# Second block of a two-block transformer kernel: the differential attention between the products that make its queries and values

## The reference

```python
def hybrid_attention_mixer(x, w_in, w_out, ...):
    proj = x @ w_in                                   # 1024 x 3072
    qa, ka, va, qb, kb, vb = split(proj)
    qa, ka, qb, kb = rms_norm of each, head by head (64 columns), times a gain
    oa = dilated_mixture_attention(qa, ka, va, slopes[:8])      # 8 heads of 64
    ob = differential_attention(qb, kb, vb, slopes[8:], lam)    # 4 heads: softmax(first) - lam * softmax(second), values 128 wide
    ob = rms_norm_2(ob, b_sub_norm) * (1.0 - lam_init)
    return concatenate([oa, ob]) @ w_out
```

## Time and profile before

| | |
|---|---|
| median of 3 runs | 2969.36 us (2969.0 to 2969.45) |
| span of the profiled execution | 2970.8 us |
| the profiled execution's own time beside it | 2970.8 us is all that is shown of it |
| TensorE busy | 2918.5 us, 98% |
| VectorE, ScalarE, GpSimd busy | 41%, 44%, 49% |
| mean granted TensorE clock | 0.995 of full |
| QKV products begin, product with w_out begins (profile) | 1759.89 us, 1979.10 us |

### The profile page before, as it was taken

The page is one execution under the profiler, slowest core; times in us unless marked ns, Lnnn a source line. Parts: engine busy times, 40 slices in busy tenths (PEclk is TensorE's granted clock), DMA queues, the critical chain, the costliest instruction groups (busy, mean ns, idle before and its releaser), DMA issues.

```text
span 2970.8 us, 39991 instructions
## 1 busy us (share of the span) xinstructions
PE 2918.5 (98%) x14264; PEld 2390.9 (80%) x14264; DVE 1232.9 (41%) x2085; ACT 1294.6 (44%) x2013; POOL 1449.4 (49%) x822
## 2 busy tenths in 40 slices
PE   8999999999989999999999999999999999999999
PEld 7878887888878778888888878668888887888887
DVE  5546434221063556433222160664555128455510
ACT  4556544222253556444223353654444237444421
POOL 4665555444444755555444454534444442444443
PEclk9999999999999999999999999999999999999999
DMA  4222232333322222333333323103333333233333
GB/s 143 73 86 78 86 121 85 99 98 100 106 78 86 75 96 65 100 114 100 96 99 99 107 78 92 58 8 101 97 99 93 99 94 92 92 98 99 93 108 89
DMA packets 77271, 273.32 MB, mean 92 GB/s; under 512 B 8776, under 2 KB 9416, under 8 KB 77152
## 3 DMA queue, kind: packets, MB, share of 16 engines
q1 hardware_dynamic: 74112, 266.05, 28.7%
q10 hardware_dynamic: 3040, 5.64, 0.5%
HBM read 269.55 MB, written 2.10 MB: 91 GB/s over the span
## 4 chain that ended last, share of the span: by engine, by line
PE 91%; DVE 4%; ACT 2%; issue 1%; POOL 1%; DMA 1%; SPq 0%; DVEq 0%; ACTq 0%; POOLq 0%
PE ps L737 25%; PE ps L739 25%; PE ps L738 25%; PE ps L1013 2%; PE ps L1038 2%; PE ps L1230 1%; PE ps L1231 1%; PE ps L1236 1%; PE ps L995 1%; DMA WRAW<-wall 1%; PE ps L1127 1%; POOL WLO L2689 1%; PE ps L1121 1%; PE ps L1122 1%; PE ps L990 0%
## 5 line engine op out<-in xcount | busy, mean ns | idle before, releaser
L2689 POOL TENSOR_TENSOR WLO<-WRAW,WHI 128x1024 fp32r<-128x1024 f32 x463 | 1116.3, 2414 | 1243.9 <-ACT WHI L1398 1243.9
L737 PE MATMUL ps<-HH,WHI 128*128 128x512 f32 x2184 | 857.2, 392 | 1.4 <-POOL WLO L2689 1.2
L739 PE MATMUL ps<-HH,WLO 128*128 128x512 f32 x2184 | 850.3, 389 | 0.0
L738 PE MATMUL ps<-HL,WHI 128*128 128x512 f32 x2184 | 850.0, 389 | 0.0
L1398 ACT ACTIVATE WHI<-WRAW 128x1024 fp32r<-128x1024 f32 x467 | 491.7, 1054 | 324.9 <-DMA WRAW<-wall 324.2
L737 PEld LDWEIGHTS ps<-HH,WHI 128*128 128x128 f32 x2184 | 410.0, 188 | 90.0 <-issue 4.8
L739 PEld LDWEIGHTS ps<-HH,WLO 128*128 128x128 f32 x2184 | 409.9, 188 | 86.3
L738 PEld LDWEIGHTS ps<-HL,WHI 128*128 128x128 f32 x2184 | 410.2, 188 | 82.7
L2535 DVE SCALAR_TENSOR_TENSOR ps<-U,COLS,ps 128x512 f32<-128x512 f32 x192 | 145.1, 756 | 121.2 <-ACT ps L1852 107.1
L2071 DVE TENSOR_TENSOR ACC<-ACC,SQ 128x512 f32<-128x512 f32 x80 | 70.5, 881 | 286.4 <-ACT SQ L1688 271.1
L737 PE MATMUL ps<-F2H,WHI 128*128 128x512 f32 x384 | 149.4, 389 | 0.0
(11 more groups left out here) (398 smaller groups left out, 4678.7 us busy)
## 6 DMA issues: line engine op xcount, KB each, us to landing
WRAW<-wall SPq DMA_DIRECT2D x502, 512.0 KB, 3.5
y<-X ACTq DMA_DIRECT2D x8, 256.0 KB, 3.9
X<-xin SPq DMA_DIRECT2D x3, 512.0 KB, 7.8
DFT<-dft ACTq DMA_DIRECT2D x4, 258.0 KB, 4.3
PT_IN<-pin ACTq DMA_DIRECT2D x2, 512.0 KB, 3.7
DIL<-dil ACTq DMA_DIRECT2D x1, 768.0 KB, 4.2
X<-xin SPq DMA_DIRECT2D x2, 256.0 KB, 4.8
COLS<-cols ACTq DMA_DIRECT2D x1, 290.5 KB, 5.5
```

The costliest lines, as they stand in the source:

```text
L737: pe.matmul(out_, WHI[w_at], x_hi, start=first, stop=False)
L738: pe.matmul(out_, WHI[w_at], x_lo, start=False, stop=False)
L739: return pe.matmul(out_, WLO[w_at], x_hi, start=False, stop=last)
L2689: pool.tensor_tensor(WLO[:, s, :], whole, WHI[:, s, :].bitcast(F32), ALU.subtract).then_inc(wt_lo, 1)
```

## The change

What it does, by engine:

- The columns of w_in are regrouped. The chunks are now: queries and keys of differential heads 0 and 1, then of heads 2 and 3, the differential values, queries and keys of dilated heads 0 to 3, then 4 to 7, and the dilated values (`QK_TILES`, "attn_w_in_2 by heads").
- `qkv` is one stage of 24 units without a loop. Its 96 steps (unit by token tile, six products each) are numbered, and tables of step numbers say between which products a piece of other work stands. All 16 differential pairs are scored, transposed and multiplied there, their norm is done head by head, and the scores of 8 of the 16 dilated pairs too. `alone` holds the last 8 dilated pairs, with the first half of four w_out tiles, now the differential half, between them.
- The order of pairs is turned round: differential first.
- The head norms are taken chunk by chunk: GpSimd's power (128 x 16, eight times) replaces square root and reciprocal, and the factors lie in SBUF (FQ) instead of PSUM.
- Within the products, all transposes (tiles, maps, spread factors) and the sums of squares use the one bank ps6, each waiting until the one before it was read (`turn_free`); from pair 20 on, second maps use ps3. All output goes to bank ps7 instead of two banks. Scores have two banks up to pair 24, four after it (before: four).
- The maps' buffers: 16 turned maps instead of 8, half of them in the parts of QKV that are no longer needed.

The core of the diff (`qkv` and `alone` as TensorE has them; `head_factors` is GpSimd's, `normed` VectorE's):

```diff
-TURNED = 8
+TURNED = 16
+QK_TILES = [f for a, h in ((8, 0), (8, 2), (0, 0), (0, 2)) for f in (a + h, a + h + 4, a + h + 1, a + h + 5)]
+QK_TURNED = by_step(24, 25, 26, 27, 40, 41, 42, 43, 73, 74, 75, 76, 89, 90, 91, 92)
+SCORED = by_step(27, 29, 32, 34, 37, 39, 42, 44, 47, 49, 52, 54, 57, 59, 62, 64, 77, 78, 80, 82, 85, 87, 89, 95)
+DIFF_TURNED = by_step(33, 35, 38, 39, 44, 45, 48, 50, 53, 55, 58, 60, 63, 65, 68, 70)
+SUMMED, SPREAD = by_step(57, 62, 69, 79), by_step(61, 67, 72, 82)
...
             def qkv(st):
+                att = st.att
+                opening_rows(st)
+                for m in range(CHUNK_STEPS, STEPS_QKV):
+                    j, s = divmod(m, ST)
+                    if m in QK_TURNED:
+                        turn_qk(att, QK_TURNED[m])
+                    if m in MAP_TURNED:
+                        turn_free(att, ("map", MAP_TURNED[m]))
+                        turn_map(att, *MAP_TURNED[m])
+                    if m in SUMMED:
+                        out_sums(att, SUMMED[m])
+                    if m in SPREAD:
+                        out_spread(att, SPREAD[m])
+                    if m in SCORED:
...
+                        scores(att, SCORED[m])
+                    for q in MULTIPLIED.get(m, ()):
...
+                        value_products(att, q)
...
+                    rows_done(st, j, s, rows_of(st, j, s, (j % 4 * 2, j % 4 * 2 + 1)))
+                alone(st, att, st.res)
...
+            def alone(st, att, res):
+                scores(att, ALONE)
+                rows_copied(st, CHUNK_VA)
+                turn_map(att, ALONE - 4, 1)
+                for k in range(ALONE, 32 + 4):
+                    if ALONE < k < 32:
+                        scores(att, k)
+                    if k < 32 + 3:
+                        turn_free(att, ("map", (k - 3, 0)))
+                        turn_map(att, k - 3, 0)
...
+                    if k == 26:
+                        half_tile(res, 0, 0, 2)
...
+            def head_factors(st, c, half_):
...
+                pool.tensor_tensor(FQ[:, at], VQ[:, at], NEGH[:, :], ALU.pow).then_inc(S["qk_factors_ready"], 1)
...
+            def normed(st, c, s):
...
+                f = FQ[:, head_sums(4 * c, s)].rearrange("p (a o) -> p a o", o=1).to_broadcast([P, 8, HD])
+                dve.tensor_tensor(v, v, f, ALU.mult).then_inc(S["qk_normed"], 1)
```

More of the change, by code:

```diff
@@ L289, in attention @@
     def attention(mode, groups, out, **opt):
-        pairs, host = groups * ST, opt.get("made")
+        pairs, host = groups * ST, opt["made"]
         n = 2 * pairs
[L292 to L296, removed]
+        per = {k: n for k in ("scores_ready", "exp_ready", "probs_turned", "turned_copied", "probs_ready")}
@@ L362, in plan @@
     n = norm("X", DM, "columns")
[L363 to L371, removed]
+    v = add("qkv", 1, 24, 24, {"rows_multiplied": 6 * (ST - 1)}, op=op, norm=n)
+    v.op_hi = op_hi
+    v.att = banded()
+    v.res = residual("O2", DT, "ffn_norm_20")
+    v.res.halves = True
     def conv_ffn(l, gain):
@@ L606, in turned_at, with turn_bank, out_tile, previous_turn @@
                 return {"gqa": PTG, "mla": PT}[st.mode][:, n % 4, :]
[L607 removed]
+            i = n % TURNED
+            return PT2[:, i, :] if i < 8 else QKV[:, i % 4, (i - 8) // 4 * SEQ:((i - 8) // 4 + 1) * SEQ]
+        def turn_bank(st, n):
+            if carried(st):
+                return turn_ps[n % 2]
+            return ps[3] if n % 2 and pair_of_map(st, n) >= ALONE - 4 else ps[6]
         def score_bank(st, q, c):
[L610 removed]
+            return ps[4 + c] if carried(st) or q <= ALONE or q % 2 == 0 else ps[1 + c]
         def out_bank(st, g):
[L613 removed]
+            return ps[st.made.heads_bank()] if carried(st) else ps[7]
+        def out_tile(g):
+            return DIL_H // 2 + g if g < DIFF_H else g - DIFF_H
+        def previous_turn():
+            order, before = [], {}
+            for m in range(CHUNK_STEPS, STEPS_QKV):
+                for kind, table in (("tile", QK_TURNED), ("map", MAP_TURNED), ("sum", SUMMED), ("spread", SPREAD)):
+                    if m in table:
+                        order.append((kind, table[m]))
+            order += [("map", (q, 0)) for q in range(ALONE - 3, 32)]
+            for a, b in zip(order, order[1:]):
+                before[b] = a
+            return before
+        BEFORE = previous_turn()
+        def turn_read(st, use):
+            kind, n = use
+            if kind == "map":
+                return copied(st, map_at(st, *n))
+            return {"tile": "qk_placed", "sum": "out_mean_ready", "spread": "out_scaled"}[kind], n + 1
         def query_hi(h):
@@ L979, in scores @@
                 a, b = spans(st.mode, t)
-                if not carried(st) and q == 1:
-                    for c in range(2):
-                        pe.wait_ge(bank_free[st.bank(2 + c)], st.use(2 + c))
-                if q >= (1 if carried(st) else 2):
+                if st.mode == "banded" and t == 0:
+                    i = 2 * g + 1
+                    pe.wait_ge(S["qk_placed"], st.at("qk_placed", i + 1))
+                if q:
                     pe.wait_ge(*scores_free(st, q))
```

621 lines of the change are left out of this document (317 added, 304 removed).

## The result

The changed kernel takes 2974.56 us (median of 20 runs, 2972.69 to 2977.26), the kernel before 2970.61 (20 runs on the same chip, 2968.47 to 2972.87). The ratio is 1.0013, with an interval of 1.0007 to 1.0019: 4 us slower. The interval lies above 1, so the loss is clear of noise, though it is inside the 0.2% that I called no change; and it is 14.6 us over the forecast of 2960.

A forecast was written before the change was run, and what follows sets the result against it. TensorE, busy 98% of the span, was taken to bound the kernel. 16.3 us won less 3 of overhead and 4 of waits gave 9.3 off the span: 2961.5, in the median 2960 us, range 2957 to 2963.4.

The forecast's parts named there:

- What bounds the kernel: Whole kernel: TensorE, busy 98% of the span, so only its unneeded time and its small losses can shorten it.
- what can be won: Attention-stage excess 11.2 us, norm's low clock 3.5, wait for copies 1.6: in all 16.3 us (to 17.8).
- TensorE's overhead: Changing between products and inserted pieces on TensorE: 20.8 us against 18.1, taken as 3 us, bounds 0 and 7.
- The new waits: TensorE waiting for pieces at fixed steps between products: taken as 4 us, bounds 0.8 and 17.
- in a queue what counts is the load: Step pricing the new waits: over 155 us VectorE is loaded 82 us (53%), GpSimd 103 (67%).
- signs of a wrong forecast: Clock falling again in the last eight pairs, or products beside short pieces taking clearly over 0.3 us each.
- The collision: VectorE's two-SBUF-input instructions blocked by GpSimd: up to 63 us, some 20 expected, VectorE at 66%; forecast unchanged.
- Rival (2): Gain lost waiting for VectorE's joins behind colliding head norms: waits 14 us, 2963.4 to 2975.3, near 2968; chance 0.27.
- Rival (3): One transpose bank, ps6: some 49 uses waiting about 0.6 us each, 29 us, ending slower at 2984; chance 0.08.
- Rival (1): Schedule holds as in first block: overhead 1, waits 0.8, 14.5 to 16 us off, say 2955; chance 0.18.
- The offset: Median taken to lie 1.4 us below the profiled span of 2970.8 us, subtracted at the end.
- The range: Beside the sum: overhead 1 to 5 and waits 2 to 7 us, giving 2957 to 2963.4 us.

The follow-up runs named there:

- short_powers: Changed kernel with GpSimd's eight powers cut to four columns and head norms using one factor, so it computes something else: 2959.84 us, ratio 0.9965 to the kernel before.
- before_unrolled: Kernel before the change, with its QKV loop over the first four chunks written out on every engine: 2968.40 us, ratio 0.9993.
- two_fixes: Changed kernel with the first two chunks' head-norm factors read from PSUM and two bias tiles made five steps later: 2962.47 us, ratio 0.9975 to the kernel before.
- queue_order: all_three, plus VectorE's joins ahead of head norms and GpSimd's weight unit of step 35 moved to step 38: 2964.11 us, ratio 0.9979 to the kernel before.
- all_three: Changed kernel with PSUM factors for two chunks, one power three steps later and two biases five steps later: 2964.54 us, ratio 0.9979 to the kernel before.
- late_bias: Changed kernel with the bias tiles of dilated heads 2 and 3 made at steps 72 and 73, not 67 and 68: 2970.32 us, ratio 0.9998 to kernel before.

## Why the prediction was wrong

**What bounds the kernel** and **what can be won** held. The low clock of the last norm, the excess of the attention stage and the wait for copies are gone; short_powers, with 4.0 us of waits and none of the clock behind them, has a region of 260.5, which is 256.5 without its waits, beside the 256.3 that my list of 16.3 us leaves; without the slow starts (1.4 and 3.0) these are 255.1 and 253.3. The sums cost 0.81 to 0.95 us per eight instructions, about as forecast. One reading was wrong: before the clock fell at 1984.26, TensorE had done not only transposes and one-column sums, but also 12 products, from 1979.10 to 1981.95. The sums alone stood right in front of the fall.

**TensorE's overhead** was forecast too large: 1.2 us by my list, 1.5 from the traces, instead of 3. Beside before_unrolled, whose full-speed work is 251.2 us, it is 2.6. All of these lie within the 1 to 5 of the range. No run isolates how pieces and products overlap.

**The new waits** were the step that failed. I took 4 us; they are 12.7 with 4.5 of clock behind them, 17.2 together, just over the upper bound of 17. That is 13.2 more than forecast. The overhead gives 1.8 back and the shorter slow start 0.4, which leaves 11.0, just how far the region is above its forecast (274.35 against 263.3). Two things were wrong in it. First, "in a queue what counts is the load". VectorE and GpSimd: from 1800 to 1955 they are busy 89.0 and 90.2 us (forecast 82 and 103), so the loads were fair (VectorE's too low by 7, GpSimd's too high by 13), and from 1770 to 2000 GpSimd idles 42.2 us in front of its weight units alone. Still a tile, a joined map and a spread factor came 3 to 4 us late. The stages of the first block that I used as nearest rows have no power in front of a scaling and no head norm that a tile waits for right behind its chunk. I named the power as something they lack, and priced it by the load, not by walking along the queue. Above all I never worked out the first chunk's chain: sums, power 2.91, power 2.91, norms, first tile. Second, I costed no clock for a wait: each of the long waits can bring the clock down for 3.4 to 6.8 us. The kernel before shows that too: in its attention stage, with a clock of 0.95, half-speed stretches of 3.4 us begin at 1912.6 and 1953.5. That the clock can fall was among my signs of a wrong forecast, but only for the last eight pairs, where it did not.

**The collision** was seen, and put to the wrong account. I expected some 20 us on VectorE and a changed chance; the head norms cost 16 x (1.294 - 0.685) = 9.7 more, and the two-number instructions, which were not among my 36, 8.8. Rival (2) had the right mechanism, norms that meet weight units, and an end of 2963.4 to 2975.3, in which the result lies. But it laid the cost on eight joins at 1.74 each. What happened is one tile (3.9), one join (2.9), and one spread factor (3.4), the last mainly by its place in GpSimd's queue. Placing the factors in PSUM, as the kernel before had them, would by itself have been worth 7.3 of the 14.6 us missed.

**Rival (3)**, ps6 as the one bank of the transposes, did not happen: the waits for readers of that bank (HQ, the copies) are 0.6 us each or less, a few in all. Rival (1) did not happen either; even short_powers waits 4.0 us where it has 0.8.

**The offset** of 1.4 us between span and median was wrong as well. It was not a property of the kernel, but of the one profiled execution, which by the 2.1 us above was at the long end. What differs between executions of one kernel by 4 us stays open: in the traces the region begins between 1757.8 and 1759.9, and half-speed stretches near 880 and 1755 us are 6.8 or 10.2 long, but no run isolates it. So the forecast's miss is 11.0 us in the region, and 3.6 in that.

**The range** beside the sum was added up wrongly: overhead of 1 to 5 and waits of 2 to 7 leave 13.3 to 4.3 us, which is 2956.1 to 2965.1 and not 2957 to 2963.4. The result lies outside of both.

## What to carry to other kernels

Between products at fixed steps, an average load of 55% says nothing about a wait: walk the queue of each engine from a piece's inputs to its step, with all instructions ahead in line, at the few tight places (the first chunk, the first maps). When an instruction is moved, ask who waits for it, and what stands behind the one that waits. Keep the second input of VectorE's instructions in PSUM where GpSimd streams SBUF beside them and somebody waits for the result (7.3 us here), and put short work that is waited for ahead of long work that is not (4.2 us). two_fixes, which does only these two, beats the kernel before by about 8 us and the changed kernel by 12. Giving weight units to VectorE where it idles gained 3.0 us over queue_order, but only 0.6 over two_fixes.

## What was not expected of the hardware

- Two-number instructions on VectorE are not safe beside GpSimd's weight units: 2.18 and 2.19 us for 0.16.
- GpSimd's power does not hold VectorE up (two norms in 1.30 us within a power), while its subtraction on 128 x 1024 does (5.62). The power itself can be held: 3.46 us for 2.91 and 1.46 for 1.01, where it began beside a head norm. It costs 2.91 us for 16 columns and 1.01 for 4.
- The same subtraction takes 1.23 us on VectorE and 2.4 on GpSimd.
- Waits of about the same length differ in what follows: half-speed stretches of 6.8, 0 and 3.4 us after 3.9, 2.9 and 3.4 of waiting, and 10.2 in all_three after 3.1. In late_bias the wait of 2.9 has 3.4 us at half speed, in the changed kernel the same wait has none.
